# Transposed X in a buffer of its own, copied into XT by ScalarE; gate-up and down biases loaded separately

## The reference

```python
gu = xb @ w_gu + b_gu                      # 1024 -> 2048
gate = jnp.minimum(gu[:, :D_FF], SWIGLU_LIMIT)
up = jnp.clip(gu[:, D_FF:], -SWIGLU_LIMIT, SWIGLU_LIMIT)
act = (up + 1.0) * (gate * jax.nn.sigmoid(gate * SWIGLU_ALPHA))
y = act @ w_down + b_down                  # 1024 -> 1024
...
y = jnp.zeros((T, D), jnp.float32).at[row_token].add(yb.astype(jnp.float32) * row_gate[:, None])
```

## Time and profile before

| | us |
|---|---|
| median of 3 runs | 1427.82 |
| lowest, highest | 1425.71, 1431.71 |
| the profiled execution | 1429.38 |
| its span, first to last instruction | 1427.6 |
| TensorE matmuls busy | 1245.4 (87%) |
| VectorE busy | 523.5 (37%) |
| ScalarE busy | 223.8 (16%) |
| POOL busy | 302.9 (21%) |
| mean granted TensorE clock | 0.952 |

### The profile page before, as it was taken

The page is one execution under the profiler, slowest core; times in us unless marked ns, Lnnn a source line. Parts: engine busy times, 40 slices in busy tenths (PEclk is TensorE's granted clock), DMA queues, the critical chain, the costliest instruction groups (busy, mean ns, idle before and its releaser), DMA issues.

```text
span 1427.6 us, 30953 instructions
## 1 busy us (share of the span) xinstructions
PE 1245.4 (87%) x12281; PEld 610.6 (43%) x12282; DVE 523.5 (37%) x1230; ACT 223.8 (16%) x432; POOL 302.9 (21%) x411
## 2 busy tenths in 40 slices
PE   7989987999879988897989799997988677799885
PEld 6855457974644333232324233332333222233322
DVE  1237777442453333233233233332323322233332
ACT  3135544441100000000000001000000000001000
POOL 3000023000132222222222223222222221222222
PEclk9999989999889999899999999999999989999998
DMA  6211012019579999999999999999999999999993
GB/s 204 65 60 59 30 59 60 2 64 380 213 286 409 411 416 413 416 416 416 416 415 415 413 415 409 404 389 417 415 414 415 414 419 418 416 415 415 414 386 78
DMA packets 62355, 452.99 MB, mean 317 GB/s; under 512 B 8928, under 2 KB 31760, under 8 KB 37712
## 3 DMA queue, kind: packets, MB, share of 16 engines
q1 hardware_dynamic: 46720, 431.13, 73.0%
q0 software_dynamic: 15600, 21.38, 6.7%
HBM read 437.20 MB, written 17.17 MB: 318 GB/s over the span
## 4 chain that ended last, share of the span: by engine, by line
PE 45%; DMA 39%; DVE 7%; issue 5%; ACT 1%; POOL 1%; SPq 1%; DVEq 1%; POOLq 0%; ACTq 0%
DMA XG<-hn_scratch,IDXC 19%; DMA BDN<-in_expert_b_down 18%; PE PS L582 18%; PE PS L912 16%; PE PS L925 6%; PE PSC L582 3%; DVE XT L1235 2%; DVE GU L1244 1%; POOL IDXC L363 1%; DMA W<-in_w_in 1%; PE PS L787 1%; SPq L193 1%; DVE BDN L1260 0%; PE PS L731 0%; PE PS L721 0%
## 5 line engine op out<-in xcount | busy, mean ns | idle before, releaser
L912 PE MATMUL PS<-W,XT 128*32 128x512 f32 x5184 | 599.3, 616 | 124.1 <-DVE XT L1235 116.4
L912 PEld LDWEIGHTS PS<-W,XT 128*32 128x32 f32 x5184 | 168.7, 113 | 514.2 <-issue 395.5
L925 PE MATMUL PS<-W,AT 128*32 128x256 f32 x5184 | 294.8, 379 | 1.2 <-DVE AT L1255 1.2
L582 PE MATMUL PS<-W 128*128 128x512 f32 (+6 forms) x1068 | 273.2, 413 | 5.3 <-DVE W L1174 1.9
L925 PEld LDWEIGHTS PS<-W,AT 128*32 128x32 f32 x5184 | 170.6, 110 | 145.5 <-issue 48.5
L582 PEld LDWEIGHTS PS<-W 128*128 128x128 f32 (+1 forms) x1068 | 172.1, 195 | 86.5 <-issue 72.2
L1244 DVE TENSOR_TENSOR GU<-PS,BGU 128x512 f32<-128x512 f32 x81 | 56.0, 692 | 345.3 <-PE PS L912 341.5
L380 POOL DMA_INDIRECT acc_scratch<-Y,IDXS x81 | 130.3, 1608 | 95.9 <-ACT Y L571 93.8
L571 ACT ACTIVATE Y<-SIG,ident 128x256 f32<-128x256 f32 x81 | 41.4, 511 | 634.5 <-DMA acc_scratch<-Y,IDXS 611.7
L376 POOL COPY IDXS<-IDX 128x1 uint32 (+1 forms) x81 | 14.8, 183 | 390.4 <-DMA acc_scratch<-Y,IDXS 390.3
L366 POOL DMA_INDIRECT XG<-hn_scratch,IDXC x82 | 83.0, 1013 | 67.9 <-POOL IDXC L363 63.2
(11 more groups left out here) (228 smaller groups left out, 619.3 us busy)
## 6 DMA issues: line engine op xcount, KB each, us to landing
W<-in_expert_w_gate_up SPq DMA_DIRECT2D x128, 2048.0 KB
W<-in_expert_w_down SPq DMA_DIRECT2D x64, 2048.0 KB
W<-in_w_in SPq DMA_DIRECT2D x9, 1024.0 KB, 5.3
W<-in_x SPq DMA_DIRECT2D x8, 512.0 KB, 4.9
W<-in_w_in SPq DMA_DIRECT2D x2, 1040.0 KB, 5.3
W<-in_w_out SPq DMA_DIRECT2D x1, 2048.0 KB, 7.6
W<-in_w_out SPq DMA_DIRECT2D x2, 1024.0 KB, 9.8
acc_scratch<-W SPq DMA_DIRECT2D x4, 512.0 KB, 11.4
```

Of the source, the lines that this page charges most:

```text
L582: return pe.matmul(o, l, r, start=st, stop=sp_)
L912: last = pe.matmul(GPS[32 * j:32 * j + 32, :].rearrange("p (g n) -> p g n", g=2), XT[:, 32 * k:32 * k + 32], rhs, start=(k == 0), stop=(k ...
L925: last = pe.matmul(DPS[32 * j:32 * j + 32, :], AT[:, 32 * k:32 * k + 32], DNW[p][:, k, j * QW:(j + 1) * QW], start=(k == 0), stop=(k == KD ...
```

## The change

1. `x_turn` writes the transposed X into `XTN`, the first 256 columns of the small tile `SM`, instead of `XT`. ScalarE copies it into `XT` (`xt_copy`), after the gate-up of the block before has read `XT`. `x_turn` waits for the copy of the block before.
2. `x_turn(i + 2)` stands behind `y_evac(i - 1)`, instead of `x_turn(i + 1)` inside `activate(i)`. POOL gathers one block further ahead, and two gathers behind the last block instead of one, for which the lists get one column more (98 instead of 97).
3. Each bias has a semaphore of its own. In `reload` the gate-up bias is loaded behind the gate-up weights and ahead of the down weights (after a wait for the last bias addition of expert e-2), the down bias between the two halves of the down weights, behind the wait for `y_free`, which the second half is now behind too.
4. VectorE spreads the gate-up bias before `activate` of an expert's first block, and the down bias behind the last Y addition of the expert before and an `x_turn`.

The core of the diff; the rest changes 97 columns to 98 in tiles and views.

```diff
@@ -154,11 +154,12 @@
         OHR = RT[:, 1428:1556].rearrange("p (k e) -> p k e", k=TOPK)
         LISTS = W1[:, 20480:24576]
         OHB = LISTS[:, 0:512].rearrange("p (i e) -> p i e", e=NE)
-        B1 = LISTS[:, 0:NT * TOPK * (MAXB + 1)].rearrange("p (t k b) -> p t k b", t=NT, k=TOPK)
-        T1 = LISTS[:, 1552:3600].rearrange("p (t k m) -> p t k m", t=NT, k=TOPK)
-        GATEB = ident[:, 0:MAXB + 1]
+        B1 = LISTS[:, 0:NT * TOPK * (MAXB + 2)].rearrange("p (t k b) -> p t k b", t=NT, k=TOPK)
+        T1 = LISTS[:, 1568:3616].rearrange("p (t k m) -> p t k m", t=NT, k=TOPK)
+        GATEB = ident[:, 0:MAXB + 2]
         XGV = XG[:, :].rearrange("p (f c) -> p c f", c=NC)
-        XTV = XT[:, :].rearrange("p (c f) -> p c f", c=NC)
+        XTN = small(0, QW)
+        XTNV = XTN.rearrange("p (c f) -> p c f", c=NC)
         ACTV = GU[:, 0:QW].rearrange("p (f c) -> p c f", c=NC)
         ATV = AT[:, :].rearrange("p (c f) -> p c f", c=NC)
         PS = [ctx.enter_context(nc.psum_tensor(f"PS{i}", [P, 512], F32))[:, :] for i in range(4)]
...
@@ -189,10 +190,11 @@
         EARLY = 11
         @block.sync
         def _(sp):
-            def biases(e, p):
+            def gu_bias(e, p):
                 sp.dma_start(BGU[p][0:P:32, :].rearrange("p (g n) -> p g n", g=2),
-                             b_gu[e].rearrange("(g j n) -> j g n", g=2, j=4)).then_inc(S_(f"bias_in{p}"), 16)
-                sp.dma_start(BDN[p][0:P:32, :], b_dn[e].rearrange("(j n) -> j n", j=4)).then_inc(S_(f"bias_in{p}"), 16)
+                             b_gu[e].rearrange("(g j n) -> j g n", g=2, j=4)).then_inc(S_(f"gu_bias_in{p}"), 16)
+            def dn_bias(e, p):
+                sp.dma_start(BDN[p][0:P:32, :], b_dn[e].rearrange("(j n) -> j n", j=4)).then_inc(S_(f"dn_bias_in{p}"), 16)
             def gu_part(e, p, parts, through=None):
                 for q in parts:
                     if through is not None:
...
@@ -265,7 +267,8 @@
                     gu_part(1, 1, [3])
                     dn_part(1, 1, [0])
             sp.wait_ge(S_("bias_zeros"), 4)
-            biases(0, 0)
+            gu_bias(0, 0)
+            dn_bias(0, 0)
             sp.wait_ge(S_("outproj"), 2 * NT)
             dn_part(0, 0, [0])
             sp.wait_ge(S_("h_out"), 16 * NT)
...
@@ -279,14 +282,18 @@
             sp.wait_ge(S_("lists_done"), 2)
             sp.wait_ge(S_("gathered"), 16)
             dn_part(0, 0, [1])
-            biases(1, 1)
+            gu_bias(1, 1)
+            dn_bias(1, 1)
             dn_part(1, 1, [1])
             def reload(e, p):
                 through = sp.value_load(LASTB[0:1, bass.ds(e - 2, 1)], min_val=0, max_val=MAXB - 1) + 1
                 gu_part(e, p, range(4), through)
-                dn_part(e, p, range(2), through)
+                sp.wait_ge(S_("gu_evac"), through)
+                gu_bias(e, p)
+                dn_part(e, p, [0], through)
                 sp.wait_ge(S_("y_free"), e - 1)
-                biases(e, p)
+                dn_bias(e, p)
+                dn_part(e, p, [1], through)
             with sp.Fori(1, NE // 2) as r:
                 reload(2 * r, 0)
                 reload(2 * r + 1, 1)
...
@@ -359,14 +366,14 @@
             g.wait_ge(S_("hn_out1"), 16 * NT // 2)
             ahead = g.value_load(LASTB[0:1, NE:NE + 1], min_val=NE - 3, max_val=MAXB - 3)
             def gather(i):
-                at = within(i, MAXB, "no routing gives more than MAXB blocks, and one is gathered behind them")
+                at = within(i, MAXB + 1, "no routing gives more than MAXB blocks, and two are gathered behind them")
                 g.tensor_copy(IDXC[:, 0:1], IDX[:, bass.ds(at, 1)]).then_inc(S_("idx_cur"), 1)
                 g.wait_ge(S_("idx_cur"), i + 1)
                 g.sem_inc(S_("pool_passed"), 1)
                 g.indirect_dma_start(out=XG[:, :], out_offset=None, in_=hn_d,
                                      in_offset=bass.IndirectOffsetOnAxis(ap=IDXC[:, 0:1], axis=0)).then_inc(S_("gathered"), 16)
             def next_gather(i):
-                g.wait_ge(S_("xt_ready"), i)
+                g.wait_ge(S_("x_turned"), i)
                 g.wait_ge(S_("gathered"), i * 16)
                 gather(i)
             def scatter(i):
...
@@ -383,11 +390,12 @@
             gather(0)
             next_gather(1)
             next_gather(2)
+            next_gather(3)
             g.wait_ge(S_("h_out"), 16 * NT)
-            next_gather(3)
+            next_gather(4)
             scatter(0)
             with g.Fori(1, ahead + 1) as i:
-                next_gather(i + 3)
+                next_gather(i + 4)
                 scatter(i)
             scatter(ahead + 1)
             scatter(ahead + 2)
...
@@ -569,10 +577,19 @@
                 if not (isinstance(i, int) and i == 0):
                     a.wait_ge(S_("scattered"), i * 16)
                 a.activation(Y[:, :], SIG[:, :], ACT.Copy, scale=GATEB[:, bass.ds(at, 1)]).then_inc(S_("ys_ready"), 1)
+            def xt_copy(i):
+                a.wait_ge(S_("x_turned"), i + 1)
+                if not (isinstance(i, int) and i == 0):
+                    a.wait_ge(S_("gu_ps"), i)
+                a.activation(XT[:, :], XTN, ACT.Copy).then_inc(S_("xt_ready"), 1)
+            xt_copy(0)
+            xt_copy(1)
             sigmoid(0)
+            xt_copy(2)
             sigmoid(1)
             y_scale(0)
             with a.Fori(2, nb) as i:
+                xt_copy(i + 1)
                 sigmoid(i)
                 y_scale(i - 1)
             y_scale(last)
...
@@ -1225,17 +1242,19 @@
             link(v.reciprocal(GREC, GSUM))
             link(tt(GATE[:, :].rearrange("p (t k) -> p t k", t=NT), GATE[:, :].rearrange("p (t k) -> p t k", t=NT), bc(GREC, TOPK), ALU.mult))
             v.wait_ge(S_("list_ps"), 4 * TOPK)
-            link(ts(LPAD, PS[4][:, 0:MAXB + 1], 0.0, PM4, ALU.is_equal, ALU.mult))
-            stt(out=IDX[:, :], in0=PS[4][:, 0:MAXB + 1], scalar=PJ, in1=LPAD, op0=ALU.add, op1=ALU.add).then_inc(S_("lists_done"), 1)
+            link(ts(LPAD, PS[4][:, 0:MAXB + 2], 0.0, PM4, ALU.is_equal, ALU.mult))
+            stt(out=IDX[:, :], in0=PS[4][:, 0:MAXB + 2], scalar=PJ, in1=LPAD, op0=ALU.add, op1=ALU.add).then_inc(S_("lists_done"), 1)
             v.wait_ge(S_("tpos"), NT)
             for i in range(4 * TOPK):
                 ts(T1[:, i // TOPK, i % TOPK, :], IOM, TPOS[:, i:i + 1], GATE[:, i:i + 1], ALU.is_equal, ALU.mult).then_inc(S_("tg_ready"), 1)
             def x_turn(i):
                 v.wait_ge(S_("gathered"), (i + 1) * 16)
-                v.transpose(XTV, XGV).then_inc(S_("xt_ready"), 1)
+                if not (isinstance(i, int) and i == 0):
+                    v.wait_ge(S_("xt_ready"), i)
+                v.transpose(XTNV, XGV).then_inc(S_("x_turned"), 1)
             x_turn(0)
             v.wait_ge(S_("gl_ps"), 1)
-            v.tensor_copy(GATEB, PS[5][:, 0:MAXB + 1]).then_inc(S_("lists_done"), 1)
+            v.tensor_copy(GATEB, PS[5][:, 0:MAXB + 2]).then_inc(S_("lists_done"), 1)
             v.wait_ge(S_("lists_done"), 2)
             def activate(i, p, first):
                 v.wait_ge(S_("gu_ps"), i + 1)
...
@@ -1244,7 +1263,6 @@
                 tt(GU[:, :], GPS, BGU[p][:, :], ALU.add).then_inc(S_("gu_evac"), 1)
                 v.wait_ge(S_("gu_evac"), i + 1)
                 ts(GU[:, 0:QW], GU[:, 0:QW], LIMIT, None, ALU.min).then_inc(S_("gate_ready"), 1)
-                x_turn(i + 1)
                 ts(GU[:, QW:2 * QW], GU[:, QW:2 * QW], LIMIT, -LIMIT, ALU.min, ALU.max)
                 v.wait_ge(S_("sig_ready"), i + 1)
                 tt(SIG[:, :], SIG[:, :], GU[:, 0:QW], ALU.mult).then_inc(S_("glu"), 1)
...
@@ -1253,43 +1271,55 @@
                 v.wait_ge(S_("act_ready"), i + 1)
                 v.wait_ge(S_("d_ps"), i + 1)
                 v.transpose(ATV, ACTV).then_inc(S_("at_ready"), 1)
-            def spread_biases(e, p, rnd):
-                v.wait_ge(S_(f"bias_in{p}"), rnd)
+            def spread_gu_bias(e, p, rnd):
+                v.wait_ge(S_(f"gu_bias_in{p}"), rnd)
                 v.sem_inc(S_("bias_passed"), 1)
                 v.stream_shuffle(BGU[p][:, :], BGU[p][:, :], [0] * 32).then_inc(S_("bias_spread"), 1)
+                v.wait_ge(S_("bias_spread"), 2 * e + 1)
+            def spread_dn_bias(e, p, rnd):
+                v.wait_ge(S_(f"dn_bias_in{p}"), rnd)
+                v.sem_inc(S_("bias_passed"), 1)
                 v.stream_shuffle(BDN[p][:, :], BDN[p][:, :], [0] * 32).then_inc(S_("bias_spread"), 1)
                 v.wait_ge(S_("bias_spread"), 2 * (e + 1))
             def y_evac(i, p):
                 v.wait_ge(S_("d_ps"), i + 2)
                 tt(SIG[:, :], DPS, BDN[p][:, :], ALU.add).then_inc(S_("y_ready"), 1)
             v.memset(IDXC[:, 1:2], 0).then_inc(S_("y_ready"), 1)
-            spread_biases(0, 0, 32)
+            x_turn(1)
+            spread_gu_bias(0, 0, 16)
+            spread_dn_bias(0, 0, 16)
             activate(0, 0, True)
+            x_turn(2)
```

(13 more changed lines are left out.)

14 lines of the change are left out of this document (7 added, 7 removed).

## The result

| us | before | after |
|---|---|---|
| median of 20 runs each, beside one another | 1428.14 | 1432.57 |
| lowest, highest | 1422.92, 1431.71 | 1426.76, 1436.1 |
| ratio, with its 95% interval | | 1.0025 [1.0015, 1.0036] |
| the profiled execution, its span | 1429.38, 1427.6 | 1431.1, 1428.9 |
| first transpose of X (expert stage begins) | 412.68 | 414.21 |

The changed kernel is 4.4 us slower, 0.25% with an interval that leaves out zero. By the bound of 0.5% that is no change. The prediction was 1417.5 us with a range up to 1424.5: wrong, by 15 us, and the time lies outside the range.

A forecast was written before the change was run, and what follows sets the result against it. The prediction took the full weight stream as the bound, with gains only from its holes and the stretch after it. Stream end and scatter chain both gave about 10.3 us: 1417.5 us off the median, range 1412 to 1424.5.

The forecast's parts named there:

- the 10.3: Whole kernel: total gain in us forecast at the end, taking the span from 1427.6 to 1417.3.
- What bounds the kernel: Expert stage: weights stream without a hole, 32.1 us an expert; gains come only from holes and the stretch after the stream.
- The chain behind it keeps its steps: Scatters from block 64: scaling 10.4 us earlier, steps unchanged at 11.9 us, so block 77 is scaled at 1381.1.
- The single step of 12.2 us: Scatter chain: one step shown, a gather 2.1 us ahead of its scatter, called no longer than the mean one.
- Removes the holes: -3.3: Weight stream, 850 to 950 us: the early start removes its holes, ending the stream 3.3 us sooner.
- The start: Start of the expert stage: transpose then copy, and block 1's early transpose, cost +0.7 us, bounds -0.2 and +2.2.
- The X part at nothing: X staged in XTN and copied by ScalarE: copy lies beside the down matmuls, VectorE's transpose waits cost 0.
- POOL's order: Gather i+4 ahead of scatter i: scatter up to 1.5 us later where Y isn't scatter-bound; 0 at the end.
- The landing of the biases and the first scaling: Expert 26: gate-up weights land at 1218.7, block 64 is scaled at 1226.0 against 1236.38, 10.4 us earlier.
- near 1380: Sign of being right: VectorE spreads the gate-up bias of expert 31 near 1380 us.
- B: Rival, 15%: smaller gain, about 1422.5; scatter step grows 0.3 to 0.5 us or the stage's start slips 2 us.
- C: Rival, 8%: slower; on POOL the gather loop outgrows the scatter loop, every scatter waits; 1434 at 1.2 us a step.

The follow-up runs named there:

- the bias part: Kernel before plus only the gate-up bias ahead of the down weights, with own semaphores and spreads, X as before: 1425.10 us, ratio 0.9981.
- late turn: Changed kernel with block 1's X transposed behind the first bias spreads, inside block 0's activation as before: 1427.86 us, then 1431.07 in a later batch.
- two Y tiles: Kernel before with two Y buffers and two scatter index columns, so scaling waits for scatter i-2: 1427.82 us, ratio 0.9998.
- both edits: Kernel before with the early biases and a second Y buffer and scatter index column, X kept as before: 1421.64 us, ratio 0.9955.
- the dose: POOL copies the scatter's index column only after the scaled Y is there: 1436.65 us in the kernel before, 1451.51 us in the changed kernel.

## Why the prediction was wrong, by its own steps

The parts, by the means of the runs: the bias part -2.7 us (predicted -11.0, that is the 10.3 and the 0.7 of the start together); the X part on top of it, with the late turn, +4.2 (predicted 0); the early first turn +2.6 (predicted +0.7). The gaps are 8.3, 4.2 and 1.9, together the 14.4 us between the forecast gain of 10.3 and the 4.1 lost. Each has about 2 us of uncertainty, and the last two are taken across batches.

**What bounds the kernel: half right.** The rows were read rightly, the conclusion wasn't drawn far enough. A wait of 611.7 us in 72 of 80 cases with a longest of 12.1 is not only a wait beside a full stream. The scatter chain takes 12.3 us a block; the stream of before takes 160.3 us for blocks 65 to 78, 11.5 a block, and on the mean of the stage 32.1 x 32 / 81 = 12.7. With two paces this near to each other, moving one alone gains little. The sum moved the stream alone.

The failing step in full, as a table of when blocks are scaled (us in the timelines; before, the bias part alone, and after):

| block | before | bias part alone | after |
|---|---|---|---|
| 5 | 497.6 | 499.2 | 505.8 |
| 35 | 868.6 | 868.8 | 878.5 |
| 43 | 954.9 | 954.7 | 966.1 |
| 60 | 1173.4 | 1164.1 | 1179.1 |
| 64 | 1236.4 | 1225.6 | 1234.3 |
| 77 | 1391.5 | 1386.6 | 1397.0 |
| 80 | 1413.4 | 1408.9 | 1414.8 |

From block 5 to 35 all three go in step, 12.3 to 12.4 us a block. Two things bound there together: these 30 blocks take 371.0 us in before, 369.6 with the bias part, 372.3 with two Y tiles and 364.7 with both edits, the DMA at 415 GB/s in all four. Either edit alone gains next to nothing, both gain 6 us. Up to block 43 the bias part has gained nothing. It gains between blocks 43 and 64, where before had fallen behind the pace of the chain, and gives half back up to block 77.

**"The chain behind it keeps its steps": this step failed** (5.8 of the 8.3 us stand in the traces, from block 64 to 77; the two profiled executions differ by 4.5 us, the means by 2.7, and that is most of the rest). I took 155.1 / 13 = 11.9 us from the earlier trace rows as the step of the chain, and shifted it by 10.4 us. It is 12.38 in the bias part alone and (1397.01 - 1234.35) / 13 = 12.51 in after. The 11.9 held two short scatters: those of blocks 68 and 76 took 8.2 and 8.5 us to the next scaling, where the median is 11.0. The stream was somewhat thinner at 1292 us during the one (362 GB/s), and ended during the other. ScalarE in before, the first of the two:

```profile
1285.52 0.51 ACT L571 ACTIVATE Y<-SIG,ident 128x256 f32<-128x256 f32 x1 [9.20 <-DMA acc_scratch<-Y,IDXS]
...
1295.07 0.51 ACT L571 ACTIVATE Y<-SIG,ident 128x256 f32<-128x256 f32 x1 [8.43 <-DMA acc_scratch<-Y,IDXS]
```

That is a step of 9.6 us. With 11.0 for both it would have been 155.1 + 2.8 + 2.5 = 160.4, or 12.3 a step, which is what the bias part alone shows (12.38). The single step of 12.2 us was in the earlier trace rows; I set it aside for the mean, and called it no longer than the mean, though 13 times the difference is 3 us.

**"Removes the holes: -3.3": only half.** In after the hole at 940 us is gone, and there is another. Windows of after:

```profile
880.00:882.00 2.00, 2.00 (x24) 0.56 (x20) 1.93 (x5) 0.00 (x0) 1.54 (x1) 1.00 0.23 98
...
940.00:942.00 2.00, 1.92 (x36) 0.91 (x28) 0.00 (x0) 0.54 (x2) 0.18 (x1) 1.00 1.06 447
```

TensorE was busy through the whole of the window at 880 us, so it was reading late and not standing; behind the pace of the scatters, as I read it.

**The start: mis-sized by about 2 us.** The mechanism was named, with bounds of -0.2 and +2.2. The gather had been bounded by 421.66, the moment at which before used it, 7.3 us after its issue. It took 8.1. And the cost was taken from TensorE's start alone: behind that stood a granted clock of 0.50 and a queue with 10 us of work that ran dry.

**The X part at nothing: mis-sized by 4.2 us.** ScalarE's copy took 0.40 to 0.42 us, below the 0.51 taken, but the price was elsewhere. The waits behind the scaling were named, and called harmless since the gate-up stood behind the gather anyway. The staging moved the gather a block ahead, and with it took away that cover: the view of waits has ScalarE's copy, not the gather, ahead of 57 gate-ups. What is released together then runs together, and POOL's issue got longer: no row of before shows that, since little ran beside the scatters there. And of POOL's order I had written that the scatter comes up to 1.5 us later where Y is not scatter-bound, and left it out of the sum, although block 64, from which the sum ran, is such a block. It came 2.3 us later, since the copy of the scatter's index column and its wait (0.20 and 0.84 us) stand behind the gather too. These are the terms that were put at nothing; how they make the 4.2 us is not shown.

**The landing of the biases and the first scaling: right, for the bias part by itself.** Block 64 came 10.8 us earlier where 10.4 were foretold. The gate-up bias of expert 31 is spread at 1379.32 with the bias part alone ("near 1380"); in after at 1388.15, since VectorE came to it late.

**The rivals.** B, a smaller gain, had both mechanisms that failed, a step that is 0.3 to 0.5 us longer and a start that slips by 2 us; they came together and larger (13 x 0.6 = 7.6 us in after, and 2.6 for the early turn). C, the slower one by POOL's order, was there with 2.3 us at block 64 and not as the loop that binds: nearly every bound scatter is issued 1.3 us after its scaling. The Trainium skill, page "DMA: Bandwidth & Descriptors", section "Queues, rings and completion order", has descriptors of one ring consumed in order, says so of the rings of SyncE and ScalarE, and adds, what the prediction left out, that a later one may finish its write before an earlier one; no run here shows a scatter held by the gather in front of it: that of block 64 in after, issued 2.1 us behind one, took 10.9 us to the next scaling (1248.85). The rival that was missing is the one that happened: the chain just behind the bound becomes the bound.

## What to carry to other kernels

Where two paces are within a few per cent of each other (here a serial chain of scatters at 12.3 us a block, and a stream of weights at 11.5 in one stretch and 12.7 on the mean), an edit that helps one of them gains only as much as the other has slack, and a duration under load must be read with what the load was at that moment: a mean that holds a few short steps is too short for the others. Before forecasting a shift, write down when the same event of each block happens over the whole stage, and see in which stretches the kernel falls behind which chain. Ahead of a first step, with queues still short, an engine that waits in order for a transfer holds all that stands behind it: put such a wait last.

## What the runs showed of the hardware that was not expected

The issue of an indirect DMA on POOL took 1.61 us and, in the kernels in which VectorE worked all through it, on products of two tiles among others, 1.75 us, with the dose 1.85 us; one who looks for it finds it in the mean of the page's group alone.

A scatter of 128 rows took 10.9 to 11.1 us (the medians of the kernels with one Y and no dose, from issue to the next scaling) beside a stream of 416 GB/s, and 4.0 us with no stream. In between it roughly follows the stream. In before the short ones were those of blocks 35 (6.9 us), 38 (6.8), 41 (5.2), 68 (8.2) and 76 (8.5), and in each case the stream was thin within them (316, 309, 179, 362 and 33 GB/s in a window of 2 us). It is not the blocks: in after block 41's wasn't short, where the hole was gone, while block 35's took 4.1 us at 98 GB/s. Nor is it a rule: in after the scatter of block 68 took 11.0 us with 366 GB/s in one window, and that of block 76 took 10.1 with 141 and 11, and with the bias part alone block 68's took 11.1 with 375. So why the one of block 68 was short in before, with 362, stays open. Where holes in the stream shorten scatters, they give part of their loss back to the chain beside it. This was read in the traces, not tried by itself. The Trainium skill, page "DMA: Bandwidth & Descriptors", section "Queues, rings and completion order", says that a DMA engine takes turns between the queues that have work, a packet at a time; the traces agree in their direction, with 11 us beside the stream and 4.0 without it.
